# Opening of a retention and pooling encoder: the first norm's sums of squares from the turned x, by token halves

## The reference, cut to what matters

```python
def _rmsnorm(x, g):
    xf = x.astype(jnp.float32)
    return xf * lax.rsqrt(jnp.mean(xf * xf, axis=-1, keepdims=True) + EPS) * g.astype(jnp.float32)

mod = jnp.dot(jax.nn.silu(c), w_ada) + b_ada
shift1, scale1, ... = jnp.split(mod, N_MOD, axis=-1)
h = (_rmsnorm(x, g_mix) * (1.0 + scale1) + shift1).astype(dt)
proj = jnp.einsum('bsd,de->bse', h, w_in)
```

## Time and profile before

| | us |
|---|---|
| median of 3 runs | 2541.79 (2541.52 to 2545.91) |
| the profiled execution | 2541.57 |
| its span | 2539.7 |
| TensorE busy in it | 2502.0 (99%) |
| VectorE, GpSimd, ScalarE busy | 1831.7, 1747.9, 1177.1 |

### The profile page before, as it was taken

How to read it: one execution, slowest core, us unless ns; L and a number is a source line. 1 busy time by engine, 2 the same in 40 slices (tenths; PEclk the granted TensorE clock), 3 DMA queues, 4 the chain that set the end, 5 groups by cost and what they waited for, 6 DMA issues and landing times.

```text
span 2539.7 us, 34810 instructions
## 1 busy us (share of the span) xinstructions
PE 2502.0 (99%) x12660; PEld 2097.6 (83%) x12660; DVE 1831.7 (72%) x2180; ACT 1177.1 (46%) x1818; POOL 1747.9 (69%) x1172
## 2 busy tenths in 40 slices
PE   6999999999999999999999999999999999999998
PEld 3889898988788888888888889898878888888886
DVE  4989888887886666765879898887678655655334
ACT  5433333335745545555634333333465545545443
POOL 1787777767487777664767878786565877775545
PEclk9999999999999999999999999999999999999998
DMA  9124242447055445597532515152532323326664
GB/s 336 42 86 138 85 137 86 154 167 235 17 176 172 151 154 172 177 359 222 187 110 67 164 51 173 43 163 65 189 99 63 115 89 108 115 89 214 193 194 146
DMA packets 296008, 362.14 MB, mean 143 GB/s; under 512 B 17312, under 2 KB 178464, under 8 KB 295840
## 3 DMA queue, kind: packets, MB, share of 16 engines
q1 hardware_dynamic: 292960, 349.44, 42.9%
q10 hardware_dynamic: 2880, 10.49, 1.1%
HBM read 283.84 MB, written 75.50 MB: 141 GB/s over the span
## 4 chain that ended last, share of the span: by engine, by line
PE 91%; POOL 4%; DVE 2%; issue 1%; ACT 1%; SPq 0%; DMA 0%; POOLq 0%; DVEq 0%; ACTq 0%
PE ps L1121 29%; PE ps L1551 16%; PE ps L1287 16%; PE ps L1483 10%; PE ps L1182 5%; PE ps L1502 3%; PE ps L1392 3%; PE ps L1219 3%; POOL f_w L2321 1%; PE ps L1570 1%; POOL f_w L2250 1%; PE ps L1336 1%; PE ps L1605 1%; PE ps L1595 1%; PE ps L1596 1%
## 5 line engine op out<-in xcount | busy, mean ns | idle before, releaser
L2321 POOL TENSOR_TENSOR f_w<-f_ring,f_w 128x512 fp32r<-128x512 f32 x434 | 597.2, 1382 | 381.2 <-ACT f_w L1879 377.9
L1121 PE MATMUL ps<-hc_hi,f_w 128*128 128x512 f32 x2240 | 690.2, 389 | 0.8 <-ACT u_act L1941 0.5
L2250 POOL TENSOR_TENSOR f_w<-f_ring,f_w 128x512 fp32r<-128x512 f32 x282 | 462.5, 1651 | 247.2 <-ACT f_w L1672 246.5
L1121 PEld LDWEIGHTS ps<-hc_hi,f_w 128*128 128x128 f32 x2240 | 420.0, 188 | 90.2 <-ACT u_act L1941 2.1
L1121 PE MATMUL ps<-hc_lo,f_w 128*128 128x512 f32 x1120 | 435.8, 389 | 0.0
L1287 PE MATMUL ps<-act_ring,f_w 128*128 128x512 f32 x1848 | 420.7, 390 | 0.0
L1287 PEld LDWEIGHTS ps<-act_ring,f_w 128*128 128x128 f32 x1848 | 346.8, 188 | 72.9 <-issue 1.0
L1879 ACT ACTIVATE f_w<-f_ring 128x512 fp32r<-128x512 f32 x434 | 269.6, 623 | 242.5 <-POOL f_ring L2331 105.2
L1551 PE MATMUL ps<-hb,f_w 128*128 128x512 f32 x1440 | 347.4, 395 | 0.0
L1672 ACT ACTIVATE f_w<-f_ring 128x512 fp32r<-128x512 f32 x282 | 175.8, 627 | 321.8 <-POOL f_ring L2258 136.0
L1551 PEld LDWEIGHTS ps<-hb,f_w 128*128 128x128 f32 x1440 | 268.3, 188 | 61.3 <-issue 6.7
(11 more groups left out here) (259 smaller groups left out, 4055.8 us busy)
## 6 DMA issues: line engine op xcount, KB each, us to landing
f_ring<-in_w_in SPq DMA_DIRECT2D x176, 256.0 KB, 4.5
f_ring<-in_w_up SPq DMA_DIRECT2D x160, 256.0 KB, 3.4
f_ring<-gated_out SPq DMA_DIRECT2D x152, 256.0 KB, 3.0
late_rows<-in_w_late SPq DMA_DIRECT2D x64, 512.0 KB, 3.9
gated_out<-gated_up SPq DMA_DIRECT2D x44, 512.0 KB, 3.8
f_ring<-down_sums SPq DMA_DIRECT2D x88, 256.0 KB, 3.0
gated_out<-t_gated SPq DMA_DIRECT2D x22, 768.0 KB, 5.4
f_ring<-in_w_down SPq DMA_DIRECT2D x66, 256.0 KB, 3.5
```

What stands on the lines that cost most here:

```text
L1121: ins = pe.matmul(ps_row[:, half_of(bank)], a[:, cols], b, start=i in (0, 1, 3) and k == 0 and n == 0, stop=k == KQ - 1 and n == 2, skip_g ...
L2250: pool.tensor_tensor(out[:, 1, :], raw, out[:, 0, :].bitcast(F32), ALU.subtract).then_inc(mix_lo.sem, 1)
L2321: pool.tensor_tensor(piece_slot(q)[:, 1, :], piece_raw(q), piece_slot(q)[:, 0, :].bitcast(F32), ALU.subtract).then_inc(piece_lo.sem, 1)
```

## The change

For the first sequence the natural x is no longer loaded or squared. The turned x is loaded in token halves: ScalarE issues the first half's eight chunks (load_first, 256 KB each) where it issued four natural tiles, SyncE the second half's eight behind the first weight tiles. With channels on the partitions, a token's sum of squares runs over partitions, so the sums are made by TensorE: a square (128 channels by 128 tokens) as the stationary operand against one column of ones.

- First half: ScalarE squares eight chunks (square_first), TensorE makes 8 by 4 one-column products (squares_of_x) between early_product k = 1 and k = 2, VectorE adds EPS from PSUM (mean_of_x), GpSimd takes the inverse root.
- Second half: VectorE squares eight chunks (late_square) between its norm_low instructions, GpSimd adds them up in seven additions, TensorE makes 4 one-column products at n = 14 (late_squares_of_x).
- The factors are spread by four products of a broadcast column with the identity (spread_first), so VectorE's diagonal is gone for this norm. The first spreading stands behind k = 5 instead of k = 4, the second inside the eight early_product of the second round, which all stand at n = 16 now, before the wait for the second row of factors.
- VectorE scales all four first-half pieces ahead of early_part(0), where it scaled one.

```diff
             def turned_half(k):
-                sp.dma_start(xT[0][:, k, :], xt[k * P:(k + 1) * P, :]).then_inc(xt_in[k].sem, 16)
+                sp.dma_start(xT[0][:, k, half_of(1)], xt[k * P:(k + 1) * P, half_of(1)]).then_inc(xt_in[k].sem, 16)
...
             for k in range(KQ, KC):
                 early_tile(0, k)
-            turned_chunk(0)
-            turned_chunk(1)
-            second_tile(4)
-            second_tile(5)
-            turned_chunk(2)
             for j in range(2, 4):
                 mix_in(mix0, j)
-            second_tile(6)
-            second_tile(7)
-            turned_chunk(3)
+            for k in range(KC):
+                turned_half(k)
...
+            def squares_of_x():
+                for k in range(KC):
+                    pe.wait_ge(*x_squared.at(first, k + 1))
+                    for t in range(4):
+                        col = (4 + t) * HALF
+                        ins = pe.matmul(ps_row[:, col:col + 1], x_sq[:, k, t * P:(t + 1) * P], ones[:, 0:1],
+                                        start=k == 0, stop=k == KC - 1)
+                ins.then_inc(x_stat.sem, 1)
+            def late_squares_of_x():
+                pe.wait_ge(*x_low.at(first, KC - 1))
+                for t in range(4):
+                    col = 6 * HALF + t
+                    ins = pe.matmul(ps_row[:, col:col + 1], x_sq[:, 0, t * P:(t + 1) * P], ones[:, 0:1], start=True, stop=True)
+                ins.then_inc(x_stat.sem, 1)
+            def spread_first(half):
+                pe.wait_ge(*rstd_done.at(first, half + 1))
+                slot = slot_of(first, "R0")
+                for t in range(4):
+                    ins = pe.matmul(ps[:, slot, half * HALF + t * P:half * HALF + (t + 1) * P],
+                                    rstd[:, 4 * half + t:4 * half + t + 1].to_broadcast([P, P]), ident, start=True, stop=True)
+                ins.then_inc(full[slot].sem, 1)
             pe.wait_ge(sil_step, 3)
             for k in range(KC):
                 early_product(0, k)
-                if k == 4:
-                    spread_rstd(first, (0,))
+                if k == 1:
+                    squares_of_x()
+                if k == 5:
+                    spread_first(0)
             ada_turn(0)
...
                     if n == 14:
-                        spread_rstd(first, (1,))
+                        late_squares_of_x()
                     if n == 16:
+                        for k in range(KC):
+                            early_product(1, k)
+                            if k == 3:
+                                spread_first(1)
                         pe.wait_ge(*rrow_done.at(first, 2))
-                    if n in range(12, 20):
-                        early_product(1, n - 12)
...
+            def square_first(k):
+                act.wait_ge(*x_in[k].at(("first", 0, 0), 16))
+                act.activation(x_sq[:, k, :], xT[0][:, k, half_of(0)], ACT.Square,
+                               scale=D ** -0.5).then_inc(x_squared.sem, 1)
...
             for half in range(2):
-                pool.wait_ge(*x_squared.at(first, 4 * half + 4))
-                pool.tensor_scalar(x_ms[:, tiles], x_ms[:, tiles], EPS, None, ALU.add).then_inc(x_eps.sem, 1)
                 pool.wait_ge(*x_eps.at(first, half + 1))
                 inverse_root(rstd[:, tiles], x_ms[:, tiles]).then_inc(rstd_done.sem, 1)
                 if half == 0:
                     for q in range(4):
                         mix_low(("mix", 0, 0), q)
+                    for n, dst, other in Y_SUMS:
+                        pool.wait_ge(*x_squared_late.at(first, other + 1))
+                        if n:
+                            pool.wait_ge(*x_low.at(first, n))
+                        pool.tensor_tensor(x_sq[:, dst, :], x_sq[:, dst, :], x_sq[:, other, :], ALU.add).then_inc(x_low.sem, 1)
...
+            def late_square(k):
+                dve.wait_ge(*xt_in[k].at(first, 16))
+                dve.wait_ge(*x_stat.at(first, 1))
+                at_k = xT[0][:, k, half_of(1)]
+                dve.tensor_tensor(x_sq[:, k, :], at_k, at_k, ALU.mult).then_inc(x_squared_late.sem, 1)
...
             dve.wait_ge(*rrow_done.at(first, 1))
-            scale_first(0)
+            for i in range(KQ):
+                scale_first(i)
             early_part(0)
-            scale_first(1)
-            norm_low(first, 0, 0)
-            scale_first(2)
-            norm_low(first, 0, 1)
-            scale_first(3)
-            norm_low(first, 0, 2)
-            diagonal(first, (1,))
-            norm_low(first, 0, 3)
+            for i in range(KQ):
+                norm_low(first, 0, i)
+                late_square(2 * i)
+                late_square(2 * i + 1)
+            mean_of_x(1)
             dve.wait_ge(*rrow_done.at(first, 2))
```

More of the change, by code:

```diff
@@ L383, in encoder_program @@
         gated_out = nc.dram_tensor("gated_out", (N_SEQ, CHUNK_PAIRS, PRODUCTS, P, HALF), F32).ap()
-        xin = [[at(f"xin{s}_{n}", kib, [P, TT // 2, S]) for n, kib in enumerate(((128, 160), (40, 56))[s])]
-               for s in range(N_SEQ)]
-        diag = [at(f"diag{s}", (192, 88)[s], [P, S]) for s in range(N_SEQ)]
+        xin = [at(f"xin{n}", kib, [P, TT // 2, S]) for n, kib in enumerate((40, 56))]
+        x_sq = at("x_sq", 128, [P, KC, HALF])
+        diag = at("diag", 88, [P, S])
         rrow = [at(f"rrow{s}", (188, 92)[s], [P, S]) for s in range(N_SEQ)]
@@ L443, in encoder_program @@
         x_in = [tally(f"x_in{i}", 0, first=16, swap=16) for i in range(TT)]
-        x_squared = tally("x_squared", 0, first=TT, swap=TT)
+        x_squared = tally("x_squared", 0, first=KC, swap=TT)
+        x_squared_late = tally("x_squared_late", 0, first=KC)
+        x_low = tally("x_squares_added", 0, first=KC - 1)
+        x_stat = tally("x_stat_summed", 0, first=2)
         xt_in = [tally(f"xt_in{k}", 0, first=16, out=16, swap=16) for k in range(KC)]
@@ L451, in encoder_program @@
         rstd_done = tally("rstd_done", 0, first=2, mid=2, swap=1)
-        diag_done = tally("diag_done", 0, first=2, mid=2, swap=2)
+        diag_done = tally("diag_done", 0, mid=2, swap=2)
         spread = tally("rstd_spread", 0, mid=2)
@@ L734, in encoder_program, with x_tile @@
                   + [(k, 0, S) for k in range(KQ, KC)]}
-        def x_tile(seq, t):
-            return xin[seq][t // 4 if seq else 0][:, t % 4, :]
+        def x_tile(t):
+            return xin[t // 4][:, t % 4, :]
         def sq_view(ap, n):
@@ L1343, in spread_rstd @@
                     pe.wait_ge(*diag_done.at(where, b + 1))
-                    of_half = diag[1 if where[0] == "swap" else 0][:, b * HALF:(b + 1) * HALF]
+                    of_half = diag[:, b * HALF:(b + 1) * HALF]
                     pe.matmul(ps[:, slot, b * HALF:(b + 1) * HALF], ones[:, :], of_half,
@@ L1996, in _ @@
             first, mix0 = ("first", 0, 0), ("mix", 0, 0)
-            for t in range(TT // 2):
-                load_x(0, t)
+            for k in range(KC):
+                load_first(k)
             act.wait_ge(vec_in, 16)
             act.activation(sil_raw[:, :], vecT[:, R_C:R_C + 2 * KC], ACT.Tanh, scale=0.5).then_inc(sil_tanh, 1)
-            square_x(first, 0)
+            for k in range(4):
+                square_first(k)
             act.wait_ge(table_step, 1)
             act.activation(small[:, 1, :], small[:, 0, :], ACT.Exp, scale=-1.0).then_inc(table_act, 1)
-            for t in range(1, 4):
-                square_x(first, t)
+            for k in range(4, KC):
+                square_first(k)
             act.wait_ge(table_args, 1)
@@ L2010, in _ @@
             row_factors(first, 0)
+            mix_high(mix0, 2)
+            mix_high(mix0, 3)
             act.wait_ge(mod_ready, 1)
@@ L2475, in diagonal @@
             def diagonal(where, halves=(0, 1)):
-                dst = diag_mid if where[0] == "mid" else diag[1 if where[0] == "swap" else 0]
+                dst = diag_mid if where[0] == "mid" else diag
                 for b in halves:
@@ L2487, in norm_scale @@
                 k, begin, end = pieces[where[0]][i]
-                dve.wait_ge(*xt_in[k].at(where, 16))
+                if where[0] == "first" and begin == 0:
+                    dve.wait_ge(*x_in[k].at(where, 16))
+                if where[0] == "swap" or end == S:
+                    dve.wait_ge(*xt_in[k].at(where, 16))
                 at_k = xT[seq][:, k, begin:end]
@@ L2719, in _, with mean_of_x @@
             ins.then_inc(table_args, 1)
-            diagonal(first, (0,))
+            def mean_of_x(half):
+                dve.wait_ge(*x_stat.at(first, half + 1))
+                if half:
+                    dve.tensor_scalar(x_ms[:, 4:8], ps_row[:, 6 * HALF:6 * HALF + 4], 1.0 / D, EPS, ALU.mult,
+                                      ALU.add).then_inc(x_eps.sem, 1)
+                else:
+                    dve.tensor_scalar(x_ms[:, 0:4], ps_row[:, 4 * HALF::HALF], EPS, None, ALU.add).then_inc(x_eps.sem, 1)
```

(3 more changed lines are left out.)

28 lines of the change are left out of this document (8 added, 20 removed).

## The result

The changed kernel is slower, by twice what was forecast. Its median is 2567.37 us (2566.72 to 2567.82, 4 runs), against 2543.54 (2541.52 to 2545.91, 4 runs) for the kernel before beside it: +23.8 us, ratio 1.0092 (95% interval 1.0078 to 1.0105). The forecast was 2553.5 with a range to 2557.0. The profiled execution took 2567.82, its span 2566.0 (2539.7 before).

What follows compares the result with a forecast made beforehand. TensorE holds 91% of the chain, with loads bounding the opening until 24.95 us. First half 11.3 us plus second half 0.6 make 11.9, which on 2541.57 gives 2553.5 us; range 2545 to 2557.

Steps and rivals of the forecast that it cites:

- The one-column block at the lower clock: First half, TensorE between second and third w_ada product: 64 instructions at the lower clock, 1.2 GHz, taking 13.2 us.
- Full-clock rival: The first half's one-column group runs at full clock in 7.6 us; total 2545.2 us; chance 0.11.
- Its start: The one-column group starts when the second w_ada product ends, at 15.1 us; bounds 13.5 to 15.3.
- a larger share of the queues: Opening loads: w_ada tiles gain queue share as ScalarE's packets are halved, moving the group's start by -1.6 to +0.2 us.
- Four scalings at 0.65.: VectorE, first half, ahead of the rows' copy: four scalings at 0.65 us where there was one, ending at 37.0.
- What hides the rest ... The cost of these is nothing.: Second half: late squares, GpSimd additions, moved mix_low and late w_ada are hidden; cost nothing, 1 to 3 us if additions slip.
- the late sums come late: Rival, second half: GpSimd additions slow beside busy VectorE, TensorE stands at n = 14 some 2.5 us more; 2556; chance 0.08.
- Five steps of 0.7: Second half, after step 17: five steps of 0.7 us, counted with 2.75 from the turn to the next product.
- nothing is given back: After the opening: the delay goes through to the end almost whole; a 1.0 us TensorE wait can swallow at most that.
- The last sign of being wrong: After the opening: the prediction is wrong if TensorE's waits behind 70 us change by more than a microsecond.
- The load of natural x ... about 0.7 us is all that the loads can give.: Opening loads: dropping natural x brings the eighth w_ada tile no earlier; at most about 0.7 us ahead of the first product.

Runs made afterwards that it cites:

- four-product: Changed kernel with only chunk 0 of the first half's squares multiplied by ones, 4 one-column products in place of 32; ratio to the kernel before 1.0052.
- wide-product: Changed kernel with the 32 one-column products made 128 columns wide, same stationary squares; median 18.3 us over the kernel before.
- filled kernel: Kernel before with eleven throw-away 512-column products on TensorE around the first turn of the adaptive rows, before the first product; ratio to the kernel before 1.0001.
- the sums on GpSimd without late additions: Changed kernel with first-half sums added on GpSimd, late squares on ScalarE, the second half's seven additions left out; ratio to the kernel before 1.0016.

## Why the prediction was wrong

The sign, the place and the main term were right. Of the 11.9 us that were missing, 3.6 stand ahead of the first product and 7.8 between it and step 23; about half of the whole is one term that was put at nothing, the late sums.

- **The one-column block at the lower clock.** Forecast 13.2 us, measured 13.8 (64 instructions at 0.214, weight loads of 333 ns as forecast). The four-product and the wide-product kernels show that it was on the path and that its clock was the cause. Full-clock rival refuted.
- **Its start.** Forecast 15.1, measured 16.44 (1.3 later). The step that failed is "a larger share of the queues": eight issues on ScalarE's queue took 5.66 us and made w_ada later, not earlier. Four issues put the tile back and the block at 15.44, so 1.0 of the 1.3 is theirs.
- **"Four scalings at 0.65."** 4.63 us instead of 2.6, because mix_low had been moved next to them. I had moved mix_low in the text, and had asked only whether it ended in time, not what ran beside it. These three terms and 0.4 less from the block to the row of factors make 40.8 into 44.4.
- **"What hides the rest ... The cost of these is nothing."** This is the step that made the forecast fail. Squares on VectorE and additions on GpSimd alternate at 1.7 us each instead of 0.65 and 1.3. TensorE waited 3.13 us, and the clock fell in that wait. From the first product to step 23 it took 35.4 us instead of 27.6: wait 3.1; late sums, six products and four w_ada products at the lower clock 3.0; 15 products behind the bunched w_ada ones 1.6; 0.6 from the second turn to the next product; 0.2 in small terms; and 0.7 less at the start. Late squares on ScalarE took out 5.6 of it, and in the three kernels without a wait at the late sums the six products behind them took 1.65 us, in the seven with one (2.4 to 4.1 us) 2.91. The rival "the late sums come late" was there, at 0.08 and 2.5 us. Its mechanism was right, its price lacked the clock.
- **"Five steps of 0.7"**, the 15 products behind the bunched w_ada ones: 5.1 us instead of 3.5. This is not the late sums' doing: with the late squares on ScalarE the clock falls at the same place. The forecast had priced the wait for the second factors, but not the clock behind it.
- **That nothing is given back** behind 80 us: right (23.25 at step 23, 23.22 a group later). The last sign of being wrong, waits behind 70 us that change by more than a microsecond, did come up in the profile (1.58 us in the output products), at a place where other kernels vary as well.
- **"The load of natural x ... about 0.7 us is all that the loads can give."** No run takes the load away alone, so for the first product this stays an argument. Behind it the filled kernel shows that a load does bound the kernel before once TensorE is faster: the turned chunk of k = 3, until 35.4 us. Whether 4 MB less would have brought it earlier was not tried.

What stays open: the three us that the sums on GpSimd without late additions still lose against the kernel before at step 23 are first product 2.5 and stretch 0.5. The stretch is 1.9 lost beside GpSimd and 1.4 gained ahead of it. Which of the spreading's place and the later w_ada tiles makes the 2.5 was not separated: the copy of the rows stands at 27.92, and both the four scalings (from 25.50) and the eighth w_ada product (until 27.50) end just ahead of it. Why the clock fell behind a wait of 2.67 us in one kernel and not in another is open too.

## What to carry to other kernels

When work moves between engines, list for each moved instruction what runs beside it, not only whether it ends in time: VectorE instructions with two SBUF inputs beside GpSimd ones slow both engines: here a square went from 0.65 to 1.7 us and an addition from 1.3 to 1.7. A sum over partitions by one-column f32 products costs two weight loads for each product, and 64 of these in a row left TensorE at 1.2 GHz, so add up first and multiply once, if an engine has the time for the additions. Price a new TensorE wait at itself plus the slow products behind it: here a wait of 3.1 us brought 3.0 us more right behind it.

## What the runs showed of the hardware

- One-column f32 products ran 13.7 us without a gap and the clock did not rise; the same products with 128 columns went from 12 to 21 instructions in 2 us at 22 us, and the block took 9.8 us in all.
- The clock view says 1.00 ahead of its first recorded change, while instructions go at 0.214 us instead of 0.11: durations tell the clock there.
- Eight 256 KB issues on ScalarE's queue took 5.66 us, four of 512 KB 2.26.
- Four VectorE scalings took 4.63 us beside two GpSimd subtractions, 5.70 with an addition as well, and 2.50 with GpSimd quiet.
